# Half-block products inside the up-projection of a recurrent decoder layer, their weight sums on GpSimd

## The chip, the cores and the metric

The kernel runs on one core of a Trainium2 chip. The metric is the device time of one execution in microseconds (us). A difference of 0.5% (11 us here) is about what a measurement of this kernel can tell from no change.

## The reference, cut to what matters

One decoder layer is applied to 1024 prompt rows and 32 decode rows (8 sequences of 4 tokens), all in float32. Three token mixers read one input projection; their outputs are gated, merged and projected. Then comes the part that the change touches, the feed-forward block (ConvFFN):

```python
h2 = modulate(h_res, p['g_ffn'], sh2, sc2)        # rows x 1024
up = h2 @ p['w_up']                               # rows x 5632, two halves of D_FF = 2816
buf = jnp.concatenate([st_conv[layer], up], axis=1)
conv = causal_dwconv(buf, p['conv_w'], p['conv_b'], l)   # 3 taps over the rows, per channel
a_ff, b_ff = jnp.split(conv, 2, axis=-1)
h_res = h_res + gt2[:, None, :] * ((jax.nn.gelu(a_ff) * b_ff) @ p['w_down'])
out_conv.append(buf[:, -(CONV_W - 1):])
```

The layer returns the rows, the states of the mixers and the last two rows of `buf` for each sequence.

## The kernel before, in words

Everything lies transposed: channels on the 128 partitions, the 1056 rows (T) along the free axis. The order of the work is written out by hand for each engine, in one program per engine that waits on semaphores. TensorE is `pe`, VectorE is `dve`, ScalarE is `act`, GpSimd is `pool`, and `sp` issues most loads.

The up-projection has 44 tiles of 128 output channels, worked off in 22 pairs `r`. Pair 2n holds two tiles of the a half (through GELU), pair 2n+1 the two tiles of the b half for the same channels. Two pairs are a group `n` of four tiles, whose weights are one load (chunk `("up", 2n)`) into one of two slots of `W`. There are 11 groups: 0 to 4, then the down-projection of that half (`down_pair`, four times), then groups 5 to 10 and the down-projection again (`HALVES`).

A pair is a product of a 2x2 matrix of weight blocks (tile x half of the 1024 inputs) with a 2x2 matrix of input blocks (half of the inputs x half of the rows). It is done with seven block products in place of eight (Strassen's scheme in Winograd's form). `multiply` is one block product: four input tiles times two column groups of 264, so eight matmuls, into two PSUM banks. The products are, in the order of `pair`: A11 B11, S2 BT2, A12 B21, A21 BT3 (A21 holds a difference by then), S1 BT1, A22 BT4, S4 B22. VectorE forms the weight sums S1, S2, S4 and the new A21 (`sums`, four operations of 512 elements a pair) and puts the products together with five additions of 528 elements out of PSUM (`combined`, counted in `comb`); ScalarE copies two products out (`p12_ev`).

VectorE then runs the three taps over each tile (`conv(r, a)`: one tensor_scalar and two scalar_tensor_tensor of 1024 elements, the same on 32 decode elements, and for b tiles the multiplication with the GELU of the a tile). The taps of pair r-1 run among the additions of pair r. ScalarE places decode rows and states (`decode_rows`), takes out the last rows (`state_rows`, `rows_out`) and does the GELU. GpSimd does nothing in this part but issue the stores of the conv rows, and before it those of the mixers' states and of the residual stream (`out`, L762).

At the end of a half, `down_pair(half, 0)` needs differences of the FFN tiles: T1 (ready early), T2 and T3, which VectorE forms after the taps of the last pair (`dn_sums`). Its first product needs neither.

Lines of the profile: L830 is a matmul and L834 a transpose of TensorE; L2274, L2277 and L2894 are VectorE's tensor_tensor, scalar_tensor_tensor and tensor_scalar; L1861 is a copy by ScalarE and L2207 its GELU.

Of the kernel before, what the change touches and what calls it, by code (L numbers as in the profile page):

```python
# [22 lines left out]
DS = 4  # L23
# [25 lines left out]
PRODUCTS = 7  # L49
N_SMALL = 24  # L50
# [22 lines left out]

def weight_chunks():
# [10 lines left out]
    for m0, m1 in HALVES:  # L85
        out += [("up", m, 2 * PRODUCTS) for m in range(m0, m1, 2)]
        out += [("down", (m0, c), PRODUCTS) for c in range(4)]
# [3 lines left out]
def trunk(nc, I, O):  # L91
# [5 lines left out]
    with ctx:  # L97
# [11 lines left out]
        hones = sb("hones", [P, P])  # L109
        m_ar = sb("m_ar", [P, 2, RCH])  # L110
        m_lt = sb("m_lt", [P, LEVELS, RCH])
        m_l0 = sb("m_l0", [P, RCH])
        idS = sb("idS", [P, RCH])
        m4 = sb("m4", [P, NS])

        resets = sb("resets", [P, T], BF16)
        shT = sb("shT", [P, RT, NS])
        shO = sb("shO", [P, RT, NSEQ])
        st5 = sb("st5", [P, 2, NJ, NS])
        ls5 = sb("ls5", [P, 2, NJ, NSEQ])  # L120
# [306 lines left out]

        def slots(r):

            return [2 * ((x - r) % 3) for x in range(3)]  # L430
# [65 lines left out]
        T1_MADE, T2_EARLY, T2_MADE, T3_MADE, T4_MADE = 1, 6, 7, 8, 9  # L496

        def down_sum(half, c, n):

            return DOWN_SUMS * half + n + (1 if c == 0 else 9 + 4 * (c - 1))  # L500
# [7 lines left out]
        def p12_of(r, n):  # L508
            return 4 + 2 * r + n + (4 if r >= HALVES[0][1] else 0)

        def p1_moved(half, c):
            return 4 + 2 * HALVES[half][1] + 4 * half + c + 1
# [5 lines left out]
        def _(sp):  # L518
# [73 lines left out]
            sp.wait_ge(sem("hg_stored"), 128)  # L592
            for lo, hi, nm in ((0, 32, "rw_w2"), (32, 64, "rw_a2"), (64, 128, "rw_g2")):
                sp.dma_start(Lw[lo:hi, :], I[nm][0]).then_inc(sem("mixer_in"), 16)
            for j in range(4):
                if j:
                    sp.wait_ge(sem("ry_done"), 2 * j)
                    weights(index[("rkv", j)])
                    sp.wait_ge(sem("rw_stored"), 64 * j)
# [9 lines left out]
            for k in range(3):  # L609
                sp.wait_ge(sem(f"gate_saved{k}"), 16 * 24)  # L610
# [55 lines left out]
        def _(pool):  # L666
            done = [0]

            def step(ins):
                done[0] += 1  # L670
                ins.then_inc(sem("pool_step"), 1)
                pool.wait_ge(sem("pool_step"), done[0])
# [85 lines left out]
            stored = {}  # L758

            def out(name, dst, src):  # L760
                stored[name] = stored.get(name, 0) + 16
                pool.dma_start(dst, src).then_inc(sem(name), 16)  # L762

            pool.wait_ge(sem("s5_rows"), 4)
            flat = s5out.rearrange("p a b c -> p (a b c)")
            out("row_stored", O["s5_p"].rearrange("l n g p c -> (l n) (g p c)"), flat[0:1, :])
            out("row_stored", O["s5_s"].rearrange("l n g p c -> (l n) (g p c)"), flat[1:NSEQ, :])
            for t in range(2):
                pool.wait_ge(sem("u_ev"), t + 1)
                for h in range(2):  # L770
                    hp = slice(64 * h, 64 * h + 64)
                    out("hg_stored", O["hg_p"][0, 0, 2 * t + h], Sc[hp, NC - 1, :])
                    out("hg_stored", O["hg_s"][0][:, 2 * t + h].rearrange("n k v -> k n v"), Sdo[hp, :, :])
            for j in range(4):
# [11 lines left out]
                pool.wait_ge(sem("rw_rows"), 2 * (j + 1))  # L786
                for h in range(2):
                    hp = slice(64 * h, 64 * h + 64)
                    out("rw_stored", O["rw_p"][0, 0, 2 * j + h], SO[hp, 8, :])
# [2333 lines left out]
```

## Time and profile before

| what | value |
|---|---|
| median of 3 runs | 2218.21 us (2211.7 to 2219.84) |
| profiled execution, first to last instruction | 2213.4 us |
| TensorE busy | 2158.7 us, 98% of the span |
| VectorE busy | 1155.9 us, 52% |
| ScalarE busy | 395.1 us, 18% |
| GpSimd busy | 161.7 us, 7% |
| mean granted TensorE clock | 0.992 |

The page gives no time of the profiled execution beside its span. A float32 matmul appears as two instructions in the records, so one block product of eight matmuls is a row with x16.

### The profile page before, as it was taken

What the parts mean: (1) busy time and instruction counts of PE and PEld (TensorE: products, weight loads), DVE (VectorE), ACT (ScalarE), POOL (GpSimd) and SP (SyncE); (2) the same over time, 40 slices, a digit from 0 to 9 for tenths busy, and PEclk for the clock granted to TensorE, in tenths of its full rate; (3) what the DMA queues carried; (4) which work ended last, traced back from release to release, by engine and by line L of the source; (5) the groups of instructions that cost most, each with busy time, mean ns of one, the idle gap of its engine ahead of it and who ended that gap; (6) DMA issues with size and microseconds to landing.
All of it is one profiled execution on the core that took longest, in us unless ns stands there. A gap on an engine that the chain in (4) does not pass through costs nothing.

```text
span 2213.4 us, 42598 instructions
## 1 busy us (share of the span) xinstructions
PE 2158.7 (98%) x18879; PEld 1608.1 (73%) x18879; DVE 1155.9 (52%) x1788; ACT 395.1 (18%) x765; POOL 161.7 (7%) x276
## 2 busy tenths in 40 slices
PE   6999999999999999999999999999999999999999
PEld 4666666666666666666666787888888888888887
DVE  5876344253353443344335667666663366666745
ACT  3122121232232132142110003111100011111001
POOL 2520000001002002001000000000000000000000
PEclk8999999999999999999999999999999999999999
DMA  8310142301211111111245222111122311110302
GB/s 289 128 44 12 56 147 81 86 12 51 64 37 57 47 52 57 47 55 37 71 165 196 88 80 75 39 41 40 45 81 89 117 40 40 40 40 30 136 30 79
DMA packets 117541, 161.57 MB, mean 73 GB/s; under 512 B 15890, under 2 KB 87047, under 8 KB 117344
## 3 DMA queue, kind: packets, MB, share of 16 engines
q1 hardware_dynamic: 101568, 132.68, 18.5%
q10 hardware_dynamic: 10992, 15.21, 1.9%
q0 software_dynamic: 4800, 10.97, 1.5%
q8 instruction: 150, 2.46, 0.5%
q14 instruction: 31, 0.25, 0.0%
HBM read 126.24 MB, written 32.59 MB: 72 GB/s over the span
## 4 chain that ended last, share of the span: by engine, by line
PE 94%; DVE 2%; issue 1%; SPq 1%; DMA 1%; ACT 1%; DVEq 0%
PE ps L830 93%; PE ps L834 1%; DVE hT L2274 1%; SPq L523 1%; DVE arena L2274 0%; ACT hT L2168 0%; DMA arena<-in_state_s_dram 0%; SPq L540 0%; DVE Y L2277 0%; DMA hT<-gates 0%; DMA gates<-arena 0%; DVE Y L2274 0%; ACT arena L1861 0%; DVE arena L2506 0%; DVE Y L2894 0%
## 5 line engine op out<-in xcount | busy, mean ns | idle before, releaser
L830 PE MATMUL ps<-hT,W 128*128 128x352 f32 (+1 forms) x3472 | 1000.2, 441 | 7.2 <-ACT hT L2168 2.3
L830 PEld LDWEIGHTS ps<-hT,W 128*128 128x128 f32 x3472 | 649.9, 191 | 274.6 <-issue 19.7
L830 PE MATMUL ps<-arena 64*64 64x64 f32 (+6 forms) x9032 | 405.0, 246 | 19.7 <-issue 17.3
L830 PEld LDWEIGHTS ps<-arena 64*64 64x64 f32 (+2 forms) x9032 | 320.3, 139 | 131.1 <-issue 79.1
L830 PE MATMUL ps<-arena,W 128*128 128x264 f32 x1200 | 278.1, 386 | 0.0
L830 PEld LDWEIGHTS ps<-arena,W 128*128 128x128 f32 x1200 | 228.0, 190 | 39.1
L2274 DVE TENSOR_TENSOR Y<-Y,ps 128x528 f32<-128x528 f32 x152 | 107.0, 704 | 270.0 <-PE ps L830 269.3
L2274 DVE TENSOR_TENSOR arena<-arena 128x1056 f32<-128x1056 f32 (+7 forms) x164 | 146.6, 894 | 58.1 <-PE ps L830 43.8
L1861 ACT ACTIVATE Y<-ps 128x528 f32<-128x528 f32 (+1 forms) x96 | 39.8, 414 | 743.4 <-PE ps L830 391.1
L830 PE MATMUL ps<-Y,W 128*128 128x352 f32 (+1 forms) x592 | 164.3, 434 | 2.0 <-DVE Y L2274 1.3
L830 PEld LDWEIGHTS ps<-Y,W 128*128 128x128 f32 x592 | 112.0, 190 | 49.8 <-DVE Y L2274 1.8
L1861 ACT ACTIVATE arena<-ps 128x512 f32<-128x512 f32 (+6 forms) x143 | 86.6, 616 | 343.7 <-PE ps L830 282.3
L762 POOL DMA_DIRECT2D out_dram<-arena x72 | 39.7, 558 | 1169.5 <-ACT arena L1861 920.9
L2274 DVE TENSOR_TENSOR arena<-ps,arena 128x512 f32<-128x512 f32 (+4 forms) x97 | 68.5, 706 | 95.7 <-PE ps L830 60.0
L783 POOL TENSOR_TENSOR arena<-arena,m_lt 128x512 f32<-128x512 f32 x40 | 50.5, 1270 | 404.0 <-DVE flag L2745 296.8
L830 PEld LDWEIGHTS ps<-idS,arena 64*64 64x64 f32 x2912 | 58.2, 135 | 19.5 <-issue 14.3
L2277 DVE SCALAR_TENSOR_TENSOR arena<-Y,PAR,arena 128x1024 f32<-128x1024 f32 (+1 forms) x88 | 67.6, 768 | 3.1
L2277 DVE SCALAR_TENSOR_TENSOR Y<-Y,PAR 128x1024 f32<-128x1024 f32 (+1 forms) x88 | 67.6, 768 | 3.1
L830 PE MATMUL ps<-hT,arena 128*128 128x264 f32 x288 | 67.2, 387 | 1.5 <-ACT hT L2168 1.5
L830 PE MATMUL ps<-idS,arena 64*64 64x64 f32 x2912 | 66.4, 221 | 0.8 <-ACT arena L1938 0.8
L1988 ACT ACTIVATE arena<-ps 128x352 f32<-128x352 f32 x72 | 33.2, 461 | 182.6 <-PE ps L830 182.5
L830 PEld LDWEIGHTS ps<-hT,arena 128*128 128x128 f32 x288 | 54.6, 190 | 11.5 <-issue 1.9
(312 smaller groups left out, 1480.4 us busy)
## 6 DMA issues: line engine op xcount, KB each, us to landing
W<-in_w_up_dram SPq DMA_DIRECT2D x22, 1024.0 KB, 6.6
W<-in_w_ada_dram SPq DMA_DIRECT2D x8, 2048.0 KB, 10.6
W<-in_w_in_dram SPq DMA_DIRECT2D x13, 1024.0 KB, 7.0
gates<-arena ACTq DMA_DIRECT2D x72, 176.0 KB, 1.8
arena<-xres SPq DMA_DIRECT2D x22, 528.0 KB, 5.1
arena<-gates SPq DMA_DIRECT2D x21, 528.0 KB, 3.6
xres<-arena POOLq DMA_DIRECT2D x16, 528.0 KB, 6.9
W<-in_w_ada_dram SPq DMA_DIRECT2D x32, 256.0 KB, 2.8
```

The costliest lines, as they stand in the source:

```text
L523: sp.dma_start(dst, src).then_inc(sem("small_in"), 16)
L762: pool.dma_start(dst, src).then_inc(sem(name), 16)
L783: pool.tensor_tensor(LT[:, 8 * s:8 * s + 8, :], LA[:, 8 * s:8 * s + 8, 0, :], m_lt[:, l, :].unsqueeze(1).to_broadcast([P, 8, RCH]), MUL)\
L830: return nc.tensor.matmul(out, lhsT, rhs, start=start, stop=stop, skip_group_check=True)
L834: return nc.tensor.transpose(out, in_, ident[0:n, 0:n])
L1861: return nc.scalar.activation(out, in_, ACT.Copy)
L1988: nc.scalar.activation(stage, bank[:, 0:GW], ACT.Sigmoid).then_inc(sem("gate_ev"), 1)
L2274: return v.tensor_tensor(out, a, b, op)
L2277: return v.scalar_tensor_tensor(out=out, in0=a, scalar=s, in1=b, op0=op0, op1=op1)
```

## The change

Nine of the eleven groups (all but 0 and 5, the first of each half) are done by a new function. Products 6, 7 and 4 of the scheme (S2 BT2, A21 BT3, A22 BT4) are taken for both pairs of a group together, as one 256 x 512 by 512 x 528 product, and this is done again with seven products of half blocks: each is two matmuls of 264 columns into a single bank (banks 4 to 7). The other four products of each pair stay as they were (banks 0 to 3).

```diff
+SUB_ORDER = (1, 6, 7, 5, 2, 4, 3)
+SUBBED = (6, 7, 4)
+def two_level(n):
+    return 2 * n not in (HALVES[0][0], HALVES[1][0])
...
+            def sub_level(n, x):
...
+                def sub(b, A, B, first=True, last=True):
+                    for k in range(2):
+                        m = mm(pb[b][:, 0:HG], A[:, k, :], B[:, k, :], first and k == 0, last and k == 1)
+                    m.then_inc(sem("gemm_done"), 1)
+
+                pe.wait_ge(sem("w_sums"), w_sum(n, {6: 8, 7: 12, 4: 20}[x]))
+                take(4)
+                sub(4, x11, y11, True, False)
+                take(5)
+                sub(5, s2, t2)
+                take(6)
+                sub(6, s3, t3)
+                take(7)
+                sub(7, s1, t1, True, False)
+                pe.wait_ge(sem("sub_copied"), 2 * kk + 1)
+                sub(4, x12, y21, False, True)
+                pe.wait_ge(sem("sub_ev"), 5 * kk + 1)
+                sub(5, x22, y12)
+                pe.wait_ge(sem("sub_ev"), 5 * kk + 3)
+                sub(7, s4, y22, False, True)
+            def two_level_group(n):
+                sub_level(n, 6)
+                multiply(0, A11, B11, True, False)
+                sub_level(n, 7)
+                multiply(0, A12, B21, False, True)
+                multiply(2, S1, BT1, True, False)
+                sub_level(n, 4)
+                multiply(2, S4, B22, False, True)
+                states_turned(n)
...
+                multiply(0, A11, B11, True, False)
+                last_rows(n - 1)
+                multiply(2, S1, BT1, True, False)
+                multiply(0, A12, B21, False, True)
+                multiply(2, S4, B22, False, True)
```

GpSimd makes all weight sums of these groups, each waiting for the one before (20 operations a group), mostly during the group before; twice it also makes or undoes sums of inputs for the second level. VectorE no longer makes weight sums there and gets 15 additions of 264 elements a group (`sub_first`, `sub_second`), ScalarE six copies of 264.

```diff
+            def w_step(out, a, b, op):
+                pool.tensor_tensor(out, a, b, op).then_inc(sem("w_sums"), 1)
+                pool.wait_ge(sem("w_sums"), done["w"])
+            def sub_set(n, x):
+                w_step(s3, x11, x21, SUB)
+                w_step(s2, x22, s3, SUB)
+                w_step(s1, s2, x11, ADD)
+                w_step(s4, x12, s2, SUB)
+            def sub_first(n, x):
+                dve.wait_ge(sem("sub_copied"), 2 * kk + 1)
+                dve.wait_ge(sem("gemm_done"), sub_product(n, x, 6))
+                step(tt(q12, q11, pb[5][:, 0:HG], ADD), "sub_ev")
+                step(tt(q21, q12, pb[6][:, 0:HG], ADD), "sub_ev")
+                step(tt(q22, q21, pb[7][:, 0:HG], ADD), "sub_ev")
+            def sub_second(n, x):
+                step(tt(q21, q21, pb[5][:, 0:HG], SUB), "sub_ev")
+                step(tt(q12, q12, pb[7][:, 0:HG], ADD), "sub_ev")
```

All stores that GpSimd issued are now issued by ScalarE, at the places where their data are ready; the last two of the residual stream stand between the root of the RMSNorm and its scaling (`x_kept_back`). T1 of the first down product is now formed by VectorE in the last group of a half, ahead of its last addition, where it stood in the pair before. Small constants and states of the mixers share one tensor with the new sums, and some semaphores are merged.

```diff
+            half_root(1)
+            x_kept_back(KT - 2, KT - 1)
...
-                    if r == m1 - 2:
-                        step(tt(down_t1(half, 0, 4), down_in(half, 0, 1, 0, 4), down_in(half, 0, 0, 0, 4), SUB))
-                        step(tt(down_t1(half, 4, K), down_in(half, 0, 1, 4, K), down_in(half, 0, 0, 4, K), SUB), "dn_sums")
...
+                if last:
+                    down_sums(half, 0, 2, 4)
+                    first_t1(half)
+                flat(O_, 3, c12, c12, 2, ADD)
```

How the order moves, TensorE first: a product of a plain pair before, and the second set of half-block products of a group after.

```order
L830 MATMUL ps<-hT,W 128x264 [waits comb,w_in1]
L830 MATMUL ps<-hT,W 128x264 x7
L830 MATMUL ps<-arena 128x264 [waits s_sums,comb]
L830 MATMUL ps<-arena 128x264 x7
L830 MATMUL ps<-hT,W 128x264 [waits p12_ev]
L830 MATMUL ps<-hT,W 128x264 x7
```

```order
L949 MATMUL ps<-arena,W 128x264 [waits sub_copied]
L949 MATMUL ps<-arena,W 128x264
L949 MATMUL ps<-arena,W 128x264 [waits sub_ev]
L949 MATMUL ps<-arena,W 128x264
L949 MATMUL ps<-arena 128x264 [waits sub_ev]
L949 MATMUL ps<-arena 128x264
L949 MATMUL ps<-hT,W 128x264 [waits comb]
L949 MATMUL ps<-hT,W 128x264 x7
```

Where TensorE waited once for eight matmuls, it now waits for every two, and what it waits for (`sub_ev`) is VectorE's addition of a product four places back.

VectorE with the taps of the pair before, first in a plain pair before the change, then in the second set of half-block products:

```order
L2894 TENSOR_SCALAR arena<-Y,PAR 128x1024 [waits comb]
L2277 SCALAR_TENSOR_TENSOR arena<-Y,PAR,arena 128x1024 [waits dve_step] x2
L2894 TENSOR_SCALAR arena<-Y,PAR 128x32 [waits u_in,dve_step]
L2277 SCALAR_TENSOR_TENSOR arena<-Y,PAR,arena 128x32 [waits dve_step] x2
L2902 MEMSET res_t 128x1 [waits u_used]
L2274 TENSOR_TENSOR Y<-Y,ps 128x528 [waits gemm_done,conv_a]
```

```order
L2550 SCALAR_TENSOR_TENSOR Y<-Y,PAR 128x1024 [waits comb]
L2550 SCALAR_TENSOR_TENSOR Y<-Y,PAR 128x1024 [waits dve_step]
L2547 TENSOR_TENSOR Y<-Y,ps 128x264 [waits gemm_done,sub_copied,dve_step]
L2547 TENSOR_TENSOR mixer<-Y,ps 128x264 [waits gemm_done,sub_ev]
L2547 TENSOR_TENSOR mixer<-mixer,ps 128x264 [waits gemm_done,sub_ev]
L3164 TENSOR_SCALAR Y<-Y,PAR 128x32 [waits u_in,sub_ev]
```

Two taps of 1024 elements stand directly ahead of the addition that lets the sixth product of the set begin.

VectorE at the end of the first half, before and then after:

```order
L2274 TENSOR_TENSOR W<-W 128x5x128 [waits w_in1,comb]
L2274 TENSOR_TENSOR arena<-W 128x640 [waits dn_sums]
L2274 TENSOR_TENSOR Y<-Y,ps 128x528 [waits gemm_done,dn_sums]
L2274 TENSOR_TENSOR Y<-Y,ps 128x528 [waits gemm_done,comb]
L2274 TENSOR_TENSOR Y<-arena 128x1584 [waits cob_made,comb]
```

```order
L3188 MEMSET res_t 128x1 [waits u_used]
L2547 TENSOR_TENSOR W<-W 128x5x128 [waits w_in1,conv_a]
L2547 TENSOR_TENSOR arena<-W 128x640 [waits dn_sums]
L2547 TENSOR_TENSOR arena<-arena 128x2112 [waits dn_sums]
L2547 TENSOR_TENSOR Y<-arena 128x528 [waits dve_step]
L2547 TENSOR_TENSOR Y<-Y,ps 128x528 [waits gemm_done,dn_sums]
L2547 TENSOR_TENSOR Y<-arena 128x1584 [waits cob_made,comb]
```

The sums for the down-projection and T1 (128x2112 and 128x528) now all stand between the taps of the a tiles and the last addition.

## Rows read from the trace of the kernel before

**Rows 1.** The page: busy time; the chain that ended last.

```profile
PE 2158.7 (98%) x18879; PEld 1608.1 (73%) x18879; DVE 1155.9 (52%) x1788; ACT 395.1 (18%) x765; POOL 161.7 (7%) x276
...
PE 94%; DVE 2%; issue 1%; SPq 1%; DMA 1%; ACT 1%; DVEq 0%
```

**Rows 2.** Windows of the up-projection (busy us and counts, then clock, DMA).

```profile
1450.00:1500.00 50.00, 50.00 (x230) 42.44 (x230) 31.17 (x45) 6.50 (x23) 2.01 (x4) 1.00 0.14 44
```

**Rows 3.** Timeline of TensorE in one group (start, us, idle before).

```profile
1585.97 3.72 PE L830 MATMUL ps<-hT,arena 128*128 128x264 f32 x16
1589.53 0.95 PE L834 MATMUL ps<-ident,Y 128*18 128x128 f32 x8
```

**Rows 4.** Forms between 1400 and 1600 us (count, busy us, mean ns).

```profile
L2274 DVE TENSOR_TENSOR Y<-Y,ps 128x528 f32<-128x528 f32 x40 | 28.2, 704 | 67.3 <-PE ps L830 67.3
L2277 DVE SCALAR_TENSOR_TENSOR Y<-Y,PAR 128x1024 f32<-128x1024 f32 x16 | 20.5, 1284 | 0.6
L2894 DVE TENSOR_SCALAR Y<-Y,PAR 128x1024 f32<-128x1024 f32 x8 | 6.5, 813 | 0.3
```

**Rows 5.** VectorE forms between 1000 and 1100 us.

```profile
L2274 DVE TENSOR_TENSOR arena<-ps,arena 128x256 f32<-128x256 f32 x5 | 2.1, 424 | 0.3
```

**Rows 6.** Timeline of VectorE in a plain pair.

```profile
1507.67 0.69 DVE L2274 TENSOR_TENSOR W<-W 128x512 f32<-128x512 f32 x1
```

**Rows 7.** Timeline of GpSimd, 82 to 103 us and once at 1049 us.

```profile
82.86 1.63 POOL L734 TENSOR_TENSOR arena<-arena,wpw 128x128 f32<-128x128 f32 x4
...
86.29 4.01 POOL L734 TENSOR_TENSOR arena<-arena,wpw 128x256 f32<-128x256 f32 x4
...
101.01 1.90 POOL L749 TENSOR_TENSOR arena<-arena 128x1024 f32<-128x1024 f32 x1
102.99 2.68 POOL L750 TENSOR_TENSOR Y<-Y,arena 128x1024 f32<-128x1024 f32 x1
...
1049.08 1.27 POOL L783 TENSOR_TENSOR arena<-arena,m_lt 128x512 f32<-128x512 f32 x1 [2.27 <-PE ps L830]
```

**Rows 8.** Timeline of VectorE beside those of GpSimd.

```profile
87.82 4.17 DVE L2274 TENSOR_TENSOR arena<-arena 64x512 f32<-64x512 f32 x4
...
101.28 9.17 DVE L2274 TENSOR_TENSOR arena<-arena,s5v 128x512 f32<-128x512 f32 x4
```

**Rows 9.** VectorE and TensorE around the end of the first half.

```profile
1590.54 2.36 DVE L2274 TENSOR_TENSOR arena<-arena 128x2112 f32<-128x2112 f32 x1
...
1592.93 0.71 DVE L2274 TENSOR_TENSOR Y<-arena 128x528 f32<-128x528 f32 x1
...
1609.32 0.83 DVE L2274 TENSOR_TENSOR W<-W 128x640 f32<-128x640 f32 x1
...
1615.43 6.39 PE L830 MATMUL ps<-arena,W 128*128 128x264 f32 x28
...
1615.70 0.70 DVE L2274 TENSOR_TENSOR Y<-Y,ps 128x528 f32<-128x528 f32 x1 [2.86 <-PE ps L830]
...
1631.17 2.05 PE L830 MATMUL ps<-Y,W 128*128 128x264 f32 x8 [1.34 <-DVE Y L2274]
```

**Rows 10.** The same for the second half.

```profile
2061.85 1.45 DVE L2274 TENSOR_TENSOR hT<-arena,Y 128x528 f32<-128x528 f32 x2
...
2064.86 1.94 PE L830 MATMUL ps<-hT,arena 128*128 128x264 f32 x8
```

**Rows 11.** Timeline of the RMSNorm ahead of the up-projection.

```profile
1356.38 7.22 ACT L2168 ACTIVATE hT<-hT,MOD,GSC 128x528 f32<-128x528 f32 x10
1357.33 5.98 PE L830 MATMUL ps<-hT,W 128*128 128x264 f32 x14 [2.28 <-ACT hT L2168]
```

**Rows 12.** Windows of the same stretch.

```profile
1355.00:1360.00 5.00, 2.72 (x7) 2.18 (x7) 4.79 (x7) 4.88 (x8) 0.00 (x0) 0.58 0.96 302
1360.00:1365.00 5.00, 3.76 (x11) 2.59 (x9) 4.72 (x9) 5.00 (x9) 0.00 (x0) 0.73 0.40 159
```

**Rows 13.** Timeline of ScalarE's queue: what issuing a store takes.

```profile
598.12 0.33 ACTq L1990 DMA_DIRECT2D gates<-arena  x1
```

More of the change, by code:

```diff
@@ L85, in weight_chunks @@
     for m0, m1 in HALVES:
-        out += [("up", m, 2 * PRODUCTS) for m in range(m0, m1, 2)]
+        out += [("up", m, PRODUCTS * len(SUBBED) + len(FLAT_AT) if two_level(m // 2) else 2 * PRODUCTS)
+                for m in range(m0, m1, 2)]
         out += [("down", (m0, c), PRODUCTS) for c in range(4)]
@@ L508, in p12_of @@
         def p12_of(r, n):
-            return 4 + 2 * r + n + (4 if r >= HALVES[0][1] else 0)
+            return 4 + sum(1 if two_level(q // 2) else 2 for q in range(r)) + n + (4 if r >= HALVES[0][1] else 0)
         def p1_moved(half, c):
-            return 4 + 2 * HALVES[half][1] + 4 * half + c + 1
+            return p12_of(HALVES[half][1], 0) + c + 1 - (0 if half else 4)
         block = ctx.enter_context(nc.Block())
@@ L785, in _ @@
                             .then_inc(sem("lt_ready"), 1)
[L786 to L789, printed above, removed]
-                    out("rw_stored", O["rw_s"][0][:, 2 * j + h].rearrange("n v k -> v n k"), SO[hp, 0:8, :])
-            pool.wait_ge(sem("sh_rows"), 4)
-            out("row_stored", O["sh_p"].rearrange("l n c -> (l n) c"), shrow2[0:1, :])
@@ new lines, in inputs_set, with fourth_input, input_back @@
+            def inputs_set(x):
+                y11, y12, y21, y22 = sub_inputs(x)
+                t1, t2, t3 = t_sums[x]
+                w_step(t1, y12, y11, SUB)
+                w_step(t2, y22, t1, SUB)
+                w_step(t3, y22, y12, SUB)
+            def fourth_input(x, r, plain):
+                y11, y12, y21, y22 = sub_inputs(x)
+                pool.wait_ge(sem("gemm_done"), product(r, plain))
+                w_step(y12, t_sums[x][1], y21, SUB)
+            def input_back(x):
+                y11, y12, y21, y22 = sub_inputs(x)
+                w_step(y12, y22, t_sums[x][2], SUB)
@@ L2237, in _ @@
                         rows_out(FT // 2 - 1)
+                    if half == 0 and c:
+                        x_put(2 * c - 2, 2 * c - 1)
+                if half == 0:
+                    act.wait_ge(sem("res_ev"), down_ev(0, 3, 7))
+                    x_put(KT - 2, KT - 1)
             def y_out(i, half):
@@ L2902, in conv @@
                     step(v.memset(res_t[:, 0:1], 0.0), "conv_a")
+            def conv(r, a):
+                for k in range(3):
+                    prompt_tap(r, a, k)
+                decode_taps(r, a)
+                conv_end(r, a)
             def combined(r, x, out, a, b, op):
@@ L2924, in second_half, with first_t1 @@
+            def first_t1(half):
+                K = down_k(half)
+                for n in range(2) if half else ():
+                    dve.wait_ge(sem(f"x_put{n}"), 64)
+                step(tt(down_t1(half, 0, 4), down_in(half, 0, 1, 0, 4), down_in(half, 0, 0, 0, 4), SUB))
+                step(tt(down_t1(half, 4, K), down_in(half, 0, 1, 4, K), down_in(half, 0, 0, 4, K), SUB), "dn_sums")
             def second_half(home, gt, from_):
```

465 lines of the change are left out of this document (347 added, 118 removed).

## The prediction, as made before the changed kernel was run

> **What bounds the kernel now.** I read four views in this order. The page first: TensorE is busy for 98% of the span and makes 94% of the chain that ended last [rows 1], so only TensorE's work and its waits count. Then the windows of the up-projection: TensorE is busy for 50.00 of 50 us at full clock, VectorE for 31.17, ScalarE for 6.50, and GpSimd only issues stores [rows 2]. Then TensorE's timeline: a block product of eight matmuls takes 1589.53 - 1585.97 = 3.56 us, or 0.445 us a matmul, and the transposes of a group take about 0.9 us (0.95 by their row, the end of which overlaps the next product) [rows 3]. A plain group of 14 products is 14 x 3.56 + 0.9 = 50.7 us. Last, VectorE's and GpSimd's timelines early in the kernel, the only place where both work on SBUF at once [rows 7, 8]. The up-projection waits for nobody now; the question is who becomes late once every second matmul waits for an addition.
>
> **What goes.** Each of three product pairs of a group is 2 x 8 = 16 matmuls and becomes 7 x 2 = 14. That is 6 of 112 matmuls a group and 54 in nine groups: 54 x 0.445 = 24.0 us less TensorE time, all of it on the path. A group without waits would take 50.7 - 2.67 = 48.0 us.
>
> **VectorE and ScalarE, without GpSimd in the way.** VectorE loses eight sums of 512 elements a group (0.69 us each, 5.5 us) [rows 6] and gets 15 additions of 264 elements from PSUM at about 0.43 us, 6.5 us (256 elements: 0.424) [rows 5]. Its load stays at 31 to 32 us of 48. I laid the group out by the order. Say a set starts at 0. Its sixth product (bank 5) comes after five products, at 4.45 us, and wants the addition of the second, which is ready 0.27 us after that product ends (a product's reader starts 0.27 us after its end) [rows 9]. For the first set, VectorE ends the last addition of the group before at 0.97, runs two taps (0.81 and 1.28) [rows 4] and ends the three additions at about 3.6, 4.0 and 4.5: TensorE does not wait. The second set starts at 9.8 and wants its first addition by 14.2. VectorE ends the taps of the first tile at 8.8, one tap at 9.6, waits for the plain product until 10.1, adds until 10.8, does two taps until 13.4 and the addition until 13.8. So 0.4 us is left there, and 0.5 us in the wait at 9.6. The third set has no taps in it. The second half of a group has 14.2 us of products for 12 us of VectorE's work. Without GpSimd there would be no stall.
>
> **GpSimd's sums.** A group needs 8 of 512 elements and 12 of 256. Undisturbed, GpSimd takes 0.41 us for 128 elements (1.63 / 4) and 1.90 us for 1024; a straight line gives 0.62 for 256 and 1.05 for 512, while another form of 512 took 1.27 [rows 7]. That is 16 to 18 us of 48, and the sums of a group are asked for half a group ahead, so TensorE does not wait for them. The cost is another. When both engines work on SBUF they lengthen each other: VectorE's tensor_tensor of 512 elements, 0.69 us elsewhere, took 4.17 / 4 = 1.04 us against GpSimd's of 256, and 9.17 / 4 = 2.29 us against those of 1024, while one of GpSimd's grew from 1.90 to 2.68 [rows 6 to 8]. With 0.04 us between operations, each operation of GpSimd costs a waiting VectorE +0.31 us at 256 and +1.56 at 1024; on a line between, +0.73 at 512. The taps read only SBUF, so I take them to suffer alike.
>
> Where it falls: the operations for the third set start when the first set is done (6.5 us), and those of the next group's weights, four of 512, follow them until about 15 us. So from 7.5 to 13.8 us VectorE's five SBUF operations (the product with the GELU, three taps, and decode taps) meet two of the 256 kind and three of the 512 kind: 2 x 0.31 + 3 x 0.73 = 2.8 us. Of this 0.9 us is room, and I take 0.3 off as GpSimd's chain has gaps. That leaves a stall of 1.6 us in front of the second set's sixth product. It comes in seven groups, those that are followed by another such group (1 to 3, 6 to 9): 7 x 1.6 = 11.2 us. Bounds: 0 if the taps are not touched, and 4.1 us a group (29 us) if each operation of GpSimd costs its whole length.
>
> The Trainium skill ("SBUF — State Buffer", section "SBUF: two separate sides") says that VectorE and GpSimd share a port pair by an exclusive lock held for a whole instruction, and that operations of VectorE with two SBUF inputs take part in it. For 1024 elements rows 7 and 8 agree (1.56 of 1.90 us); for 256 they show half of it (0.31 of 0.62). Taken at its word it makes the second rival below.
>
> **The end of a half.** T1 and the sums for the down-projection now stand ahead of the last addition. From the end of the a pair's last product: addition 0.27 + 0.70, taps and decode taps of one tile 4.5, addition, tap, three more additions 3.8, two sums 1.7 (0.83 each), taps 3.5, two sums 1.7, T1 2.36 + 0.71 = 3.1 [rows 4, 6, 9]: the last addition can start at 19.4 us. TensorE needs 0.9 + 4 x 3.56 = 15.1 us, so it would have started at 15.4. It is 4.0 us late, and what follows on VectorE (difference, taps of two tiles, T2) has no gap. Before, TensorE waited 1.34 us there [rows 9]; this becomes 5.3. In the second half T1 and the sums are longer (+0.9, by elements), and T2 was ready at 2063.30, 1.56 us before its product at 2064.86 [rows 10]: 4.0 + 0.9 - 1.5 = 3.4 us. Together +7.4 us. VectorE could do less badly only if the two tiles' taps were not the tail; bound 4 to 10.
>
> **The clock.** Ahead of the up-projection, where TensorE idled 2.28 us and more in pieces, the granted clock of the two following windows was 0.58 and 0.73, that is 0.42 x 5 + 0.27 x 5 = 3.5 us at the lower of the two levels instead of the higher [rows 11, 12]. A wait of over 4 us at the end of the first half may do the same once, for half of that: +1.7 us; bounds 0 and 3.5 at each of two places.
>
> **The moved stores.** ScalarE pays 0.33 us for each [rows 13]. In the up-projection that is four a group, with ScalarE at 6.5 us in 50 [rows 2]: hidden, as the copy that TensorE wants next is some us away. In the mixers four come at the end of each head group, after the copies; nothing there waits for less than a microsecond of ScalarE, 0 to 9 us in all for 28 stores, taken as 0. In the RMSNorm two stand on the path, ahead of the first scaling, whose reader is TensorE [rows 11]: 2 x 0.33 = +0.7 us. The merged semaphores and the shared tensor cost nothing that a row shows.
>
> **Sum.** -24.0 + 11.2 + 7.4 + 1.7 + 0.7 = -3.0 us. The profiled span is 2213.4 us, and the page shows nothing around it; the median is 4.8 us above. -3.0 on the span is 2210.4; on the median 2218.2 it is 2215.2, and I predict 2215 us: no change that a measurement can tell (0.5% is 11 us).
>
> **Rivals.**
> *The taps are hardly touched.* Then the stall before the sixth product is gone. For it: the disturbed rows are tensor_tensor of VectorE against GpSimd operations in a row, not taps, and GpSimd's sums here wait for one another. Against: GpSimd's rows were lengthened as well, which no luck in timing explains. -24.0 + 7.4 + 0.7 = -15.9, or 2202 us. If only half the stall comes, 2208.
> *The lock is whole.* Each of GpSimd's operations delays VectorE by its length, 0.62 or 1.05 to 1.27 us: 2 x 0.62 + 3 x 1.15 = 4.7, less 0.9 of room, 3.8 us a group, 26.6 us in seven, and the stalls then come near enough to each other to lower the clock at both ends of a half (+3.5). -24.0 + 26.6 + 7.4 + 3.5 + 0.7 = +14.2, or 2232 us. It decides from about 2.2 us a group, where gain and loss are even. For it: the rows at 1024 elements. Against: those at 256.
> *ScalarE is late in the mixers.* It issues 28 more stores there; 0.33 us each, all in front of a copy that frees a bank, is 9 us: 2224 us. Against: ScalarE is busy for 18% and named for 1% of the chain [rows 1].
> *The gain is not there.* A matmul pair in a bank of its own could cost more than two eighths of a product. Against: transposes and products follow one another without a gap in rows 3. No time of its own beyond the first sum, 2218 + 15.
>
> **How the numbers follow.** Forecast 0.42, taps untouched or nearly 0.30, whole lock 0.16, ScalarE 0.08, no gain 0.04. The forecast's own range is 2207 to 2226. The range for 8 times in 10 takes in most of the first rival and the second: 2201 to 2233. Faster by over 11 us (below 2207): nearly all of the first rival and a little of the forecast, 0.33. Within: 0.44. Slower: the second rival, the last and a little of the forecast, 0.23.
>
> **What would show it.** In the changed profile TensorE's matmuls of 264 columns in a group are 212 instructions instead of 224, and groups without a wait are 48.0 us apart. A wait of 1 to 2 us for VectorE in front of one product of the second set, once in each of seven groups, shows the fourth step; VectorE's taps of 1024 elements would average above 1.284 us in the windows and GpSimd's sums above 1.05. No such wait, or taps at 1.28, says the first rival; waits of 3 us and more, also in the first set, the second. At the end of the halves I expect waits of about 5 and 3.4 us for VectorE and a granted clock under 1 behind the longer. I am wrong if TensorE waits for GpSimd's sums, or if the stretch before the up-projection changes by more than 4 us.

## The result, and the profile after

The changed kernel takes 2250.2 us (median of four runs, 2249.4 to 2255.1), the kernel before beside it 2219.0 us (2211.7 to 2221.7). The ratio is 1.0149, with a 95% interval of 1.0133 to 1.0166: 1.5% slower. The prediction said 2215 us with a range of 2201 to 2233, so it was wrong, range included. The profiled spans are 2213.4 and 2248.5 us: 35.1 us to account for. Of all executions one, in experiment 5, stood apart (2487 us at a mean granted clock of 0.85); it is in no number here.

The page of the changed kernel, busy times and chain, as in [rows 1]:

```profile
PE 2152.5 (96%) x18771; PEld 1594.1 (71%) x18771; DVE 1226.8 (55%) x1851; ACT 411.1 (18%) x812; POOL 351.2 (16%) x386
...
PE 85%; DVE 11%; issue 1%; DMA 1%; SPq 1%; ACT 1%; ACTq 0%; DVEq 0%
```

TensorE has 108 instructions less (54 matmuls of two each), as worked out. But VectorE now makes 11% of the chain instead of 2%: TensorE waits for it. TensorE's timeline has every such wait in brackets; those from 1380 to 1660 us, other rows left out:

```profile
1395.35 0.39 PE L953 MATMUL ps<-ident,Y 16*128 16x16 f32 x4 [1.00 <-DVE Y L2547]
...
1414.54 3.80 PE L949 MATMUL ps<-hT,Y 128*128 128x264 f32 x16 [0.80 <-DVE Y L2547]
...
1423.10 1.16 PE L949 MATMUL ps<-arena,Y 128*128 128x264 f32 x4 [0.32 <-DVE Y L2547]
...
1437.53 2.13 PE L949 MATMUL ps<-arena,W 128*128 128x264 f32 x4 [4.34 <-DVE Y L2547]
...
1491.78 2.13 PE L949 MATMUL ps<-arena,W 128*128 128x264 f32 x4 [3.00 <-DVE Y L2547]
...
1546.22 2.13 PE L949 MATMUL ps<-arena,W 128*128 128x264 f32 x4 [3.00 <-DVE Y L2547]
...
1597.19 1.16 PE L949 MATMUL ps<-arena,W 128*128 128x264 f32 x4 [1.13 <-DVE Y L2547]
...
1636.20 2.02 PE L949 MATMUL ps<-arena,W 128*128 128x264 f32 x8 [0.34 <-DVE Y L2547]
...
1651.60 3.68 PE L949 MATMUL ps<-Y,W 128*128 128x264 f32 x8 [5.37 <-DVE Y L2547]
```

The rows of 1437 to 1597 us are the sixth product of the second set in groups 1 to 4, the place that the prediction named. It had 1.6 us in groups 1 to 3 and 6 to 9 and nothing in 4 and 10. Groups 6 to 10 show 3.00, 3.00, 3.00, 4.36 and 1.14 there: 3.00 us and more in the seven groups that it named, and 1.1 in the other two. The nine waits make 26.0 us. The two ends of the halves make 5.37 + 0.34 and 3.25 + 0.53 us (before: 1.34 in the first, [rows 9]), and four small places 3.1 us in all (1.00, 0.80, 0.32, and 0.96 in group 6).

The second loss is the clock. Windows of the changed kernel (columns as in [rows 2], the clock is the third number from the end):

```profile
1400.00:1600.00 200.00, 187.42 (x814) 155.87 (x813) 149.69 (x201) 32.19 (x100) 94.93 (x81) 0.96 0.13 40
1600.00:1700.00 100.00, 94.28 (x419) 79.37 (x418) 64.15 (x84) 8.34 (x26) 4.26 (x3) 0.98 0.18 60
1700.00:2000.00 300.00, 285.61 (x1284) 240.18 (x1284) 184.05 (x256) 35.83 (x114) 109.28 (x91) 0.99 0.20 66
2000.00:2150.00 150.00, 145.09 (x645) 121.81 (x644) 103.09 (x134) 16.92 (x54) 12.04 (x12) 0.98 0.18 62
```

In the kernel before the same stretches are granted 1.00. Here 0.04 x 200 + 0.02 x 100 + 0.01 x 300 + 0.02 x 150 = 16 us are lost to it; the clock's own records have 30.7 us at the lower level (1.2 GHz) there, which is 15.4 us. In 3.5 of the 30.7 us TensorE stood waiting anyway, so about 13.6 us of time are lost.

A wait costs more than its bracket shows. Group 7 has one wait of 3.00 us and no time at the lower level, and by its transposes in TensorE's timeline it is 1907.83 - 1856.37 = 51.46 us long:

```profile
1856.37 0.60 PE L953 MATMUL ps<-ident,Y 128*18 128x128 f32 x4
...
1907.83 0.60 PE L953 MATMUL ps<-ident,Y 128*18 128x128 f32 x4
```

A group without a wait takes 48.16 us (experiment 1), so the wait of 3.00 us cost 3.30. Over nine groups this 0.3 is 2.7 us.

The account of the 35.1 us: -24.0 for the matmuls, +26.0 and +2.7 in the second sets, +8.2 at the ends of the halves (9.5 less the 1.34 of before), +3.1 at small places, +13.6 of clock, and 4.0 us that TensorE's work is late already at 1357 us. That is 33.6; 0.6 us arise behind the last matmul, and 0.9 us stay without a place.

### The profile page after: what moved, and what is told of

The parts are those of the page before. It is cut to its first block, busy times and chain, and to the rows that moved or that the text cites. A ratio compares the mean times of both kernels' runs of the same rounds, so it can differ in the third digit from the quotient of the medians.

```text
span 2248.5 us, 42908 instructions
## 1 busy us (share of the span) xinstructions
PE 2152.5 (96%) x18771; PEld 1594.1 (71%) x18771; DVE 1226.8 (55%) x1851; ACT 411.1 (18%) x812; POOL 351.2 (16%) x386
## 4 chain that ended last, share of the span: by engine, by line
PE 85%; DVE 11%; issue 1%; DMA 1%; SPq 1%; ACT 1%; ACTq 0%; DVEq 0%
PE ps L949 84%; DVE Y L2550 4%; DVE arena L2547 2%; DVE Y L2547 2%; DVE Y L3164 1%; PE ps L953 1%; DVE arena L2550 1%; SPq L598 1%; DMA out_dram<-arena 0%; ACT hT L2386 0%; DMA W<-in_w_in_dram 0%; DMA arena<-in_state_s_dram 0%; SPq L615 0%; DVE W L2547 0%; DVE arena L3164 0%
## 5 line engine op out<-in xcount | busy, mean ns | idle before, releaser
L949 PE MATMUL ps<-hT,W 128*128 128x352 f32 (+1 forms) x3292 | 963.5, 445 | 7.6 <-ACT hT L2386 2.7
L949 PE MATMUL ps<-arena 64*64 64x64 f32 (+7 forms) x9248 | 463.6, 249 | 20.3 <-issue 16.9
L949 PEld LDWEIGHTS ps<-arena 64*64 64x64 f32 (+3 forms) x9248 | 361.9, 140 | 139.5 <-issue 79.4
L2547 DVE TENSOR_TENSOR Y<-Y,ps 128x528 f32<-128x528 f32 (+1 forms) x161 | 98.5, 612 | 203.9 <-PE ps L949 201.5
L843 POOL TENSOR_TENSOR arena<-arena,mixer 128x512 f32<-128x512 f32 x40 | 50.6, 1273 | 883.3 <-DVE flag L3018 776.7
L2053 ACT ACTIVATE Y<-ps 128x264 f32<-128x264 f32 (+1 forms) x88 | 41.9, 476 | 622.9 <-PE ps L949 526.0
L849 POOL TENSOR_TENSOR arena<-arena 128x256 f32<-128x256 f32 (+1 forms) x30 | 35.1, 1169 | 346.7 <-DVE hT L2547 323.1
L849 POOL TENSOR_TENSOR W<-W 128x512 f32<-128x512 f32 (+1 forms) x36 | 45.0, 1250 | 267.5 <-DMA W<-in_w_up_dram 158.7
L949 PEld LDWEIGHTS ps<-mixer,arena 64*64 64x64 f32 x2912 | 58.3, 134 | 19.7 <-issue 14.5
L949 PE MATMUL ps<-mixer,arena 64*64 64x64 f32 x2912 | 66.8, 220 | 0.8 <-ACT arena L2130 0.8
```

The lines of the kernel that those rows point to most:

```text
L843: pool.tensor_tensor(LT[:, 8 * s:8 * s + 8, :], LA[:, 8 * s:8 * s + 8, 0, :], m_lt[:, l, :].unsqueeze(1).to_broadcast([P, 8, RCH]), MUL)\
L849: pool.tensor_tensor(out, a, b, op).then_inc(sem("w_sums"), 1)
L949: return nc.tensor.matmul(out, lhsT, rhs, start=start, stop=stop, skip_group_check=True)
L2053: return nc.scalar.activation(out, in_, ACT.Copy)
L2547: return v.tensor_tensor(out, a, b, op)
```

## The experiments

Up to 1093 us TensorE's work is the same in all kernels, but the span of this stretch differs by 0 to 10 us from one execution to another (matched by TensorE's instructions: -0.1 us in the changed kernel, 10.2, -0.2, 10.1 and 5.4 in the first four experiments). Much of it is the clock: experiments 1 and 3 have 41.0 us at the lower level there, the kernels before and after 27.3. So I read each experiment also from its own stages: the shift of TensorE's instructions against the kernel before that arises from 1357 us to about 2200 us. It is +30.5 us for the changed kernel. (Behind 2200 us experiments 1, 6 and 7 lose another 1.7 us to the clock, in work that is the same in all.)

**1. Almost no sums on GpSimd (e1_small_sums).**

```diff
+                if weights[0]:
+                    out, a, b = out[:, :, 0:16], a[:, :, 0:16], b[:, :, 0:16]
                 pool.tensor_tensor(out, a, b, op).then_inc(sem("w_sums"), 1)
```

> GpSimd's 20 weight sums of a group are made on 16 of their 128 columns, each with the same waits and signals (most of the weight sums are left out). Theory A (GpSimd's operations on SBUF lengthen VectorE's, and VectorE is then late for the second set): the waits of 3 us before the sixth product of the second set go in all nine groups, and with them about 12 of the 15.4 us that the granted clock costs. Of 38.5 us that TensorE waits for VectorE in these stages about 10 stay, at the ends of the halves. 2250 - 28 - 12 = 2210 us, VectorE's taps of 1024 elements back at 1.28 us. Rival B (VectorE's own order is too late, with or without GpSimd): taps get shorter, but waits of 1.5 us and more stay there; about 2235 us. Rival C (the clock falls for another reason, such as the shape of the matmul pairs): waits go and the clock still falls; 2222 us.

Measured: 2215.9 us, ratio to before 0.9987 (0.9972 to 1.0003); stage shift -8.2 us. The total is 6 us above the 2210 that was expected. The sums of inputs are still made whole. No wait is left in any second set; left are 0.71 us in group 0, 0.96 in group 6 and the two ends. Groups are 1558.38 - 1510.22 = 48.16 us apart, by the transposes in TensorE's timeline:

```profile
1510.22 0.42 PE L961 MATMUL ps<-ident,Y 16*128 16x16 f32 x4
...
1558.38 0.42 PE L961 MATMUL ps<-ident,Y 16*128 16x16 f32 x4
```

A plain group of the kernel before took 50.82, so 2.66 of the 2.67 us of the first step are there. The clock is 1.00 from 1400 to 1600 and from 1700 to 2000 us. Theory A holds; B and C fall: without GpSimd's sums VectorE's own order is in time, and the matmul pairs as such do not lower the clock.

The two timelines of VectorE side by side give the size. First the changed kernel in group 2, VectorE, then GpSimd:

```profile
1475.40 1.14 DVE L3164 TENSOR_SCALAR Y<-Y,PAR 128x1024 f32<-128x1024 f32 x1
...
1480.93 1.57 DVE L2550 SCALAR_TENSOR_TENSOR Y<-Y,PAR 128x32 f32<-128x32 f32 x2
...
1483.46 1.71 DVE L2547 TENSOR_TENSOR arena<-arena,Y 128x1056 f32<-128x1056 f32 x1
1485.21 1.64 DVE L3164 TENSOR_SCALAR Y<-Y,PAR 128x1024 f32<-128x1024 f32 x1
1486.89 0.71 DVE L2547 TENSOR_TENSOR Y<-Y,ps 128x528 f32<-128x528 f32 x1
1487.63 3.63 DVE L2550 SCALAR_TENSOR_TENSOR Y<-Y,PAR 128x1024 f32<-128x1024 f32 x2
1491.30 0.43 DVE L2547 TENSOR_TENSOR Y<-Y,ps 128x264 f32<-128x264 f32 x1
```

```profile
1474.69 1.29 POOL L849 TENSOR_TENSOR Y<-W,Y 128x512 f32<-128x512 f32 x1 [5.38 <-PE ps L949]
...
1483.33 0.72 POOL L849 TENSOR_TENSOR arena<-W,arena 128x256 f32<-128x256 f32 x1
1484.14 3.84 POOL L849 TENSOR_TENSOR W<-W 128x512 f32<-128x512 f32 x2
1488.06 2.13 POOL L849 TENSOR_TENSOR arena<-W 128x512 f32<-128x512 f32 x1
1490.26 2.15 POOL L849 TENSOR_TENSOR Y<-W 128x512 f32<-128x512 f32 x1
```

And VectorE in the same place of e1_small_sums:

```profile
1526.37 0.81 DVE L3172 TENSOR_SCALAR Y<-Y,PAR 128x1024 f32<-128x1024 f32 x1
...
1531.59 0.61 DVE L2558 SCALAR_TENSOR_TENSOR Y<-Y,PAR 128x32 f32<-128x32 f32 x2
...
1533.15 1.26 DVE L2555 TENSOR_TENSOR arena<-arena,Y 128x1056 f32<-128x1056 f32 x1
1534.45 0.81 DVE L3172 TENSOR_SCALAR Y<-Y,PAR 128x1024 f32<-128x1024 f32 x1
1535.44 0.70 DVE L2555 TENSOR_TENSOR Y<-Y,ps 128x528 f32<-128x528 f32 x1 [0.18 <-PE ps L957]
1536.18 2.61 DVE L2558 SCALAR_TENSOR_TENSOR Y<-Y,PAR 128x1024 f32<-128x1024 f32 x2
1538.82 0.43 DVE L2555 TENSOR_TENSOR Y<-Y,ps 128x264 f32<-128x264 f32 x1
```

The product with the GELU grows by 0.45 us, the tap behind it by 0.83, the other two taps by 1.02, and two decode taps of 32 elements by 0.96 (from 0.61; they take 0.54 elsewhere). One tap of the first set, beside the last of GpSimd's sums at 1474.69, grows by 0.33. That is 3.59 us. The additions that read PSUM keep their 0.43 and 0.71 us.

Now count from the start of the second set, which is at 1484.17 us in the changed kernel and at 1535.14 in e1_small_sums. The first addition of the set ends at 7.56 us instead of 4.11, so it is 3.45 us later: the 3.59 less the 0.18 us for which VectorE waited in e1_small_sums, and 0.04 of small differences. In e1_small_sums the sixth product begins at 4.45 us, 0.34 after the addition's end; when it waits for the addition it begins 0.05 us after its end. So 0.29 us was room, and the product begins 3.45 - 0.29 = 3.16 us late (7.61 instead of 4.45). The bracket shows 3.00 of it, as the row of the product in front is drawn 0.16 us longer (1.05) than the distance of the products (0.89).

**2. GpSimd's four large sums later (e2_gpsimd_late).**

```diff
+                if not behind_plain:
+                    pool.wait_ge(sem("gemm_done"), sub_product(n - 1, 7, SUB_ORDER[-1]))
                 w_step(AE[2], AE[0], AE[2], SUB)
```

> GpSimd starts the four sums of 512 elements for the next group only when the second set of this group is done, so they fall into the two plain products where VectorE is idle for 5 us. Theory A: VectorE meets only the 256 kind in front of the second set; the wait before its sixth product falls from 3 us to 0 or 0.5 in groups 2, 3 and 7 to 9, group 1 and 6 included as far as their wait is of that kind, and the clock stays at 1: 2250 - 20 - 11 = 2219 us. Rival B (VectorE's own order): nothing changes, 2250. Rival D (GpSimd's chain is then too late): TensorE waits for GpSimd's sums at the start of a set, 2235 or more.

Measured: 2226.6 us, ratio 1.0037 (1.0022 to 1.0053); stage shift +4.7 us. TensorE's timeline, groups 1 to 3:

```profile
1434.73 1.16 PE L951 MATMUL ps<-arena,W 128*128 128x264 f32 x4 [1.49 <-DVE Y L2549]
...
1484.32 1.16 PE L951 MATMUL ps<-arena,W 128*128 128x264 f32 x4 [1.14 <-DVE Y L2549]
...
1533.91 1.16 PE L951 MATMUL ps<-arena,W 128*128 128x264 f32 x4 [1.14 <-DVE Y L2549]
```

The wait falls from 3.00 to 1.14 us (in groups 1 and 9 from 4.3 to 1.49), not to 0 to 0.5: the direction was right, but what stays was put too low. In group 2 of this run the two decode taps take 1.52 us, the product with the GELU 1.72 and the tap of the first set 1.14, as in the changed kernel; the three taps behind are back at 0.82 and 1.28. That is 0.91 + 0.46 + 0.33 = 1.70 us of lengthening, less 0.18 and 0.29 of room, and the sixth product begins 5.75 instead of 4.45 us after the set's start, 1.30 late. The changed kernel has the same waits of 1.13 and 1.14 us in groups 4 and 10, which no large sums follow. Rivals B and D fall: the wait moved with GpSimd's work, and no wait for GpSimd came. The total is 8 us above the expected 2219. The windows from 1400 to 1600 and 1700 to 2000 us have a clock of 1.00: waits of 1.14 to 1.49 us once a group did not lower it.

**3. The additions ahead of the taps (e3_adds_first).**

```diff
-                prompt_tap(Q, 1, 1)
-                prompt_tap(Q, 1, 2)
                 sub_first(n, 7)
+                prompt_tap(Q, 1, 1)
+                prompt_tap(Q, 1, 2)
```

> VectorE makes the first three additions of the second set ahead of the second and third tap instead of behind them; nothing is left out and GpSimd is unchanged. If only the place of the additions counts, TensorE waits at most 0.5 us there, the clock stays up, and VectorE's lengthened taps run in its 5 us of idle time behind the set: 2250 - 20 - 11 = 2219 us. If the lengthened taps only make VectorE late for something later (the fourth and fifth addition, GELU), a wait of 1 to 3 us comes at the third set or behind it: 2235 to 2250 us.

Measured: 2219.0 us, ratio 0.9989 (0.9974 to 1.0005), as the first expectation said; stage shift -3.8 us. In the second sets two waits of 0.68 us are left (groups 1 and 9). VectorE's timeline in group 3:

```profile
1540.66 0.43 DVE L2547 TENSOR_TENSOR mixer<-mixer,ps 128x264 f32<-128x264 f32 x1
1541.13 3.62 DVE L2550 SCALAR_TENSOR_TENSOR Y<-Y,PAR 128x1024 f32<-128x1024 f32 x2
1544.78 0.58 DVE L3164 TENSOR_SCALAR Y<-Y,PAR 128x32 f32<-128x32 f32 x1
```

The taps still take 3.62 us instead of 2.61, behind the additions now, where nobody waits. So the lengthening of these taps costs nothing by itself; what cost time was the addition that stood behind them in VectorE's row.

**4. T1 early in the first half (e4_t1_early).** T1's place overlaps memory in which a part of the first set's sums stands at that time, so this kernel overwrites them; the amount of work is the same.

```diff
+                if last and half == 0:
+                    first_t1(half)
                 flat(E, 5, c22, c21, 2, ADD)
...
-                    first_t1(half)
+                    if half:
+                        first_t1(half)
```

> In the first half only, T1 (2.36 + 0.71 us on VectorE) is made in the second set of the last group, where VectorE has 5 us idle, instead of ahead of the half's last addition. My account: the wait at the end of the first half falls from 5.4 to about 2.3 us, the one of the second half stays at 3.2, and the clock drop behind the first may go: 2245 to 2247 us. Rival (something else than VectorE's length of work sets that end, as GELU): the wait stays at 5.4 and the time at 2250.

```profile
1654.56 3.54 PE L949 MATMUL ps<-Y,W 128*128 128x264 f32 x8 [2.83 <-DVE Y L2547]
```

In TensorE's timeline the wait is 2.83 us instead of 5.37, and the 0.34 us ahead of it are gone: VectorE's length of work sets that end, 2.9 us for 3.07 us of work moved. The total, 2252.6 us (2242.0 to 2254.3; ratio 1.0133, 1.0103 to 1.0162), is not the expected 2245 to 2247 and is too coarse to show a change. The stage shift is +25.4 instead of +30.5 us. Of these 5.1 us the shorter waits explain 2.9; most of the rest is that the lower level behind the end of the second half, 6.8 us in the changed kernel, did not come in this execution.

**5. The stored states (c1_adds_store).** As experiment 3, and

```diff
-            dve.wait_ge(sem("mixer_stored"), 384)
             for n in range(KT):
+                if n == 2:
+                    dve.wait_ge(sem("mixer_stored"), 384)
```

This is about the 4 us ahead of the up-projection. The chain of waits of the changed kernel between 1125 and 1156 us (start, length, what):

```profile
1133.13 0.72 ACT arena L2053 x2
...
1133.87 0.50 ACTq L2330
...
1134.41 0.64 ACTq L2331
...
1135.08 0.69 ACTq L2330
...
1135.80 9.46 DMA out_dram<-arena
...
1145.34 1.27 DVE arena L2547
```

VectorE's lifted products wait for the last states to be stored; before, GpSimd issued these, and the same operation waited for the load of the gates.

> As e3_adds_first, and VectorE waits for the mixers' stored states only ahead of the third tile of the lifted product (the first whose place overlaps them), not ahead of the first. Theory: of the 4 us by which TensorE's work is later than before at 1357 us, 3.6 to 4.0 arise between 1093 and 1149 us, in every changed kernel so far, as VectorE waits 14.1 us for stores that ScalarE issues late and slowly (0.50 to 0.69 us each); that shift goes to 0 or below, and the time from 2219 to 2215 us. Rival (the load of the lift weights or gates is what ends there, as in the kernel before): a shift of 2 us or more stays.

Measured: 2211.3 us, ratio 0.9971 (0.9961 to 0.9981); stage shift -4.3 us, near that of experiment 3. The shift between 1093 and 1149 us is -0.2 us, where it was +3.7 in the changed kernel and +3.8 to +4.1 in experiments 1 to 4. Of the 3.7 us about 2.1 are the later start of VectorE's operation (1145.34 instead of 1143.26), and the rest is a drop of the clock at 1146.3 us (3.4 us at the lower level), which is also gone here. VectorE waits for the gates' load again:

```profile
1144.77 1.26 DVE L2547 TENSOR_TENSOR arena<-ps,hT 128x1056 f32<-128x1056 f32 x1 [11.70 <-DMA hT<-gates]
```

**6 and 7. The end of a half (c2_tail), and GpSimd late as well (c3_late).** As experiment 5, and in the last group of each half

```diff
+                if last:
+                    t1_part(half, *(((2, 4), (4, 6)) if half else ((0, 2), (3, 4), (4, 5))))
                 flat(E, 5, c22, c21, 2, ADD)
+                if last:
+                    down_sums(half, 0, 0, 1 if half else 2)
                 sub_first(n, 4)
```

> As c1_adds_store, and in the last group of each half four fifths (two thirds in the second half) of T1 and two (one) of the four sums for the down-projection are made in the second set, where VectorE idles, instead of behind the third. 2.4 + 1.7 us leave VectorE's chain at the end of the first half and about 2.4 + 1.0 at that of the second. If VectorE's length of work sets both ends, the waits fall from 5.4 to about 1.4 and from 3.3 to about 0, and with them some of the clock's loss there (now 6.8 us at half clock at each, 3.4 us each): 2215 - 7 - 4 = 2204 us. Rival (TensorE's transposes or ScalarE's GELU are next in line there): waits of 3 and 2 us stay, 2211 us.

> As c2_tail, and GpSimd starts the next group's four sums of 512 elements only behind the second set, as in e2_gpsimd_late. If the additions in front of the taps have already taken all of it off TensorE's path, nothing is gained but the 0.7 us in group 1: same time as c2_tail within 1 us. If GpSimd's chain becomes late for a third set's weights, waits for GpSimd appear and it is slower than c2_tail.

Measured: c2_tail 2201.0 us (2198.5 to 2204.0), ratio 0.9930 (0.9918 to 0.9942), stage shift -16.0; c3_late 2199.4 us, ratio 0.9918 (0.9905 to 0.9931), stage shift -18.0. In c2_tail the end of the first half waits 1.85 us (1.4 expected) and the second 0.64 + 0.50 (0 expected), and the clock behind the first stays at 1.00:

```profile
1627.83 2.05 PE L949 MATMUL ps<-Y,W 128*128 128x264 f32 x8 [1.85 <-DVE Y L2547]
```

```profile
1600.00:1700.00 100.00, 98.15 (x443) 83.16 (x442) 55.66 (x77) 6.77 (x19) 0.00 (x0) 1.00 0.24 84
```

Both are faster than the two kernels that this began with, by 0.7 and 0.8% than the kernel before. c3_late takes the two waits of 0.67 us (groups 1 and 9) away; its interval overlaps that of c2_tail, so more than that isn't shown.

**8. GpSimd's work added to the kernel before (b_gpsimd_load).**

```diff
+                pool.wait_ge(sem("gemm_done"), product(2 * n, 1))
+                for width in [256] * 4 + [512] * 4 + [256] * 8 + [512] * 4:
+                    pool.tensor_tensor(scr[:, 0:width], scr[:, 0:width], scr[:, 0:width], ADD)\
+                        .then_inc(sem("scr_step"), 1)
```

> The kernel before, with 20 operations of GpSimd added to each of the 11 groups (8 of 512 and 12 of 256 elements, each waiting for the one before, on scratch memory that nobody reads). Theory: the interference lengthens VectorE's taps here as well (mean of the scalar_tensor_tensor of 1024 elements above 1.45 us instead of 1.28), but no TensorE operation wants an addition soon, so a plain group stays at 50.7 us and the time at 2219 to 2222 us. Rival (VectorE's load as such, 31 us of 50 grown by 5 to 8 us, holds TensorE up): groups of 51.5 us and more, 2228 us or more.

Measured: 2226.8 us, ratio 1.0044 (1.0029 to 1.0059); stage shift +6.6 us. The forms of VectorE between 1390 and 2100 us:

```profile
L2287 DVE SCALAR_TENSOR_TENSOR Y<-Y,PAR 128x1024 f32<-128x1024 f32 x44 | 63.8, 1449 | 1.6
...
L2287 DVE SCALAR_TENSOR_TENSOR arena<-Y,PAR,arena 128x32 f32<-128x32 f32 x44 | 28.6, 650 | 1.6
```

Taps of 1024 elements take 1.45 us instead of 1.28 (the edge of what was expected), those of 32 elements 0.65 instead of 0.25, and plain groups stay 50.8 us apart (1543.50 - 1492.68). So the groups did as the theory said. The total did not. 1.95 us of new wait stand in group 0, where VectorE's sums of inputs (128x2112) grow from 2.36 to as much as 3.08 us and hold up a copy of ScalarE that TensorE wants. At the end of the first half TensorE waits 2.85 instead of 1.34 us, with 3.4 us at the lower level behind it. So GpSimd's work cost nothing in the plain groups, where VectorE has room, and something at two places where it has none.

## Why the prediction was wrong

Three steps failed, all in the same direction: the wait that GpSimd's sums cause (11.2 us forecast, 26.0 measured), the clock (1.7, 13.6 measured) and the moved stores (0.7, 4.0 measured at 1357 us). That VectorE is late for one product of the second set, and that GpSimd's sums make it late, was right.

- **What goes** (-24.0): right. 48.16 us a group without waits, 48.0 forecast.
- **VectorE without GpSimd in the way**: right. No stall in experiment 1. But the working found two pieces of room, "0.4 us" before the wanted addition and "0.5 us in the wait at 9.6", and added them to 0.9; measured are 0.29 us at the addition (0.34 less the 0.05 that the product takes to start) and 0.18 in the wait.
- **GpSimd's sums, the stall** (+11.2): the place and the mechanism were right, the size was not. Forecast were 2.8 us of lengthening less 0.9 of room and 0.3 for gaps, 1.6; measured are 3.59 less 0.47 of room and 0.04 more, 3.16. So about half of the miss is lengthening that was left out, and half is what was taken off. The lengthening missed at the 256 kind: two at 0.31 us were priced, and three came, 0.48 for each of the two decode taps and 0.45 for the product with the GELU. A sum of 512 beside a tap of the first set (0.33) was not in it. The three of the 512 kind cost 1.85 us, less than the 2.2 forecast. In groups 1 and 9 a third decode tap meets a sum (0.76 and 0.79 us instead of 0.30) and the product with the GELU meets one of 512 (2.25 us instead of 1.26): hence 4.34 and 4.36. And groups 4 and 10 wait 1.13 and 1.14 for the 256 kind alone, where the forecast had nothing: 26.0 us in nine groups instead of 11.2 in seven.
- **The clock** (+1.7): I expected one drop, at the end of a half. It fell behind six of the nine waits of 3 us and more (seven in second sets, two at the ends), to 30.7 us at the lower level and a loss of 13.6.
- **The second rival** came near for a wrong reason. Its waits summed to 26.6 us, close to the 26.0, but as 3.8 in each of seven groups, where the groups had 3.00 five times, 4.3 twice and 1.1 twice. It had 3.5 us of clock and nothing for the mixers, so its 2232 was still 18 us too low.
- **The last rival** is misadded: without the gain the forecast's own terms are +21.0 us, not the 15 of "2218 + 15", so its time would be 2239. It fell in any case: the gain is there.
- **The ends of the halves** (+7.4): right, 8.2 measured, and experiments 4 and 6 show that it is VectorE's length of work.
- **The moved stores** (+0.7): the step said that nothing in the mixers waits for ScalarE's time. It priced issuing alone. The landing is waited for, by VectorE: +3.7 us between 1093 and 1149 us with the clock behind it, gone in experiment 5. The two stores in the RMSNorm lengthen TensorE's waits there from 2.28 and 1.48 to 2.66 and 2.42 us, 1.3 us instead of 0.7; shorter time at the lower level in that stretch (3.4 us instead of 6.8) hides 0.9 of it in this pair of executions. The change ahead of the up-projection is 4.0 us, at the bound that the prediction set itself.
- **Not foreseen**: 3.1 us of small waits in groups 0, 1 and 6. In group 0 (1.00 us) GpSimd makes its first sums of inputs (528 elements) beside VectorE's own weight sums, which grow from 0.69 to between 1.18 and 1.68 us; in experiment 1, where the sums of inputs stay, 0.71 of it stays. The 0.80 and 0.32 us of group 1 are gone in experiment 1. The 0.96 us of group 6 stay in every experiment on the changed kernel, so they are not GpSimd's: the first set follows the last plain product at once and wants VectorE's addition of it, 0.27 + 0.70 us.
- **The rule in dispute.** I weighed that VectorE and GpSimd lock a shared port for a whole instruction (the Trainium skill, "SBUF — State Buffer", section "SBUF: two separate sides") against rows in which 256 elements cost half their length, and gave it 0.16. The trace of the changed kernel agrees with the rule, for small and long operations alike, and shows two things more: the engines take turns, and the next one begins 0.11 to 0.26 us before the end that the trace shows for the other (table in the last section). So an operation of VectorE pays for what is left of GpSimd's sum in progress, and GpSimd pays the rest: from 1484.14 to 1492.41 us its four sums of 1.27 us took 2.17, 1.60, 2.13 and 2.15, 2.97 us more, and VectorE's three taps lost 1.85. The rival's price, a whole length for each sum, was too high for the 512 kind: a tap loses only the rest of a sum, and while VectorE adds from PSUM (0.71 us of that time) a sum runs on at nobody's cost. The forecast priced each sum at less than its length, which was right in kind; it counted too few of the 256 kind.

## What to carry to other kernels

An engine with idle time over a group can still be late at one place: lay its row out up to each addition that is wanted soon, and put what reads PSUM and is wanted next ahead of the long work on SBUF; that one swap was worth 31 us here (2250.2 to 2219.0). Lengthening by a second engine belongs in that layout as a delay of everything queued behind it, small operations included: an operation of 0.25 us lost twice its own length here. And a wait on TensorE's path is priced with the clock that may fall behind it: here 13.6 us behind 38.5 us of waits, about a third more.

## What the runs showed of the hardware

- VectorE and GpSimd took turns on SBUF. These are all operations of both from 1483.4 to 1492.5 us in the changed kernel that have their data in SBUF alone (the timeline merges two of one kind; here they stand apart). Taken alone, they last 1.26 (product with the GELU), 0.81 (tensor_scalar), 1.28 (scalar_tensor_tensor) and 1.27 us (sum of 512). If each does its own work at the end of the time shown, it begins that work here:

| operation | start | us | alone | begins its work | the other engine's operation in front ends |
|---|---|---|---|---|---|
| VectorE, product with the GELU | 1483.46 | 1.71 | 1.26 | 1483.91 | 1484.06 |
| GpSimd, sum of 512 | 1484.14 | 2.17 | 1.27 | 1485.03 | 1485.17 |
| VectorE, tensor_scalar | 1485.21 | 1.64 | 0.81 | 1486.04 | 1486.30 |
| GpSimd, sum of 512 | 1486.38 | 1.60 | 1.27 | 1486.71 | 1486.85 |
| VectorE, scalar_tensor_tensor | 1487.63 | 1.43 | 1.28 | 1487.78 | 1487.98 |
| GpSimd, sum of 512 | 1488.06 | 2.13 | 1.27 | 1488.91 | 1489.06 |
| VectorE, scalar_tensor_tensor | 1489.10 | 2.17 | 1.28 | 1489.98 | 1490.18 |
| GpSimd, sum of 512 | 1490.26 | 2.15 | 1.27 | 1491.15 | 1491.26 |

  Each begins 0.11 to 0.26 us before the other's shown end. The two decode taps fit as well: 0.77 us each beside sums that end at 1481.65 and 1482.45, with 0.25 of work that begins at 1481.45 and 1482.25.
- GpSimd's tensor_tensor on SBUF takes 0.72 us for 256 elements and 1.27 for 512 when undisturbed (0.62 and 1.05 to 1.27 in the forecast), and up to 2.17 us beside VectorE's taps. With all operands in one tensor (experiment 8) it takes 0.61 and 1.04. VectorE's operations with one operand in PSUM kept their time beside it (0.43 us for 264, 0.70 for 528 elements).
- The same wait of 3.00 us lowered the granted clock in the first half and not in the second. Windows of the changed kernel:

```profile
1490.00:1515.00 25.00, 23.22 (x92) 19.16 (x93) 11.55 (x20) 2.34 (x8) 10.82 (x11) 0.86 0.00 1
1830.00:1855.00 25.00, 22.00 (x100) 18.14 (x100) 14.38 (x22) 2.57 (x9) 13.73 (x12) 1.00 0.01 2
```

  Why is open; no run here tells it.
- ScalarE took 0.50 to 0.69 us to issue a store of a RWKV state, against 0.33 for one of the gates [rows 13], and the last of them landed 9.46 us after its issue.
